# One copy and one guard for both heads in the attention core, and a norm's last square summed by TensorE

## What is computed

```python
def rmsnorm(x, g):
    y = x * lax.rsqrt(jnp.mean(x * x, axis=-1, keepdims=True) + EPS)
    return y * g

def attend_block(qb, keys, values, masks, sink):
    m = sink
    for s in scores:                       # 128 queries against up to 512 keys
        m = jnp.maximum(m, jnp.max(s, axis=-1))
    denom = jnp.exp(sink - m)
    for s, vp in zip(scores, values):
        p = jnp.exp(s - m[..., None])
        denom = denom + jnp.sum(p, axis=-1)
        out = out + p @ vp
    return out / denom

for i in range(4):                         # attention, pooling, Fourier, attention
    x = x + g1 * mixer_i(modulate(rmsnorm(x, norm_mix[i]), sh1, sc1))
    x = x + g2 * conv_ffn(modulate(rmsnorm(x, norm_ffn[i]), sh2, sc2))
```

## Time and profile before

| | |
|---|---|
| median of 3 runs | 2660.65 us (2658.5 to 2661.7) |
| the profiled execution | 2665.53 us, its span 2663.7 us |
| PE busy | 2573.9 us (97%) |
| DVE busy | 1984.8 us (75%) |
| ACT busy | 1299.1 us (49%) |
| POOL busy | 115.5 us (4%) |
| mean granted TensorE clock | 0.984 of full |

### The profile page before, as it was taken

One profiled execution on the slowest core, in us unless ns is written; L12 is line 12 of the kernel. 1 busy time (PEld: TensorE's weight loads), 2 busy tenths in 40 slices (PEclk: granted clock), 3 DMA queues, 4 the chain that ended last, 5 costly groups with the idle time before them and its releaser, 6 DMA issues.

```text
span 2663.7 us, 43103 instructions
## 1 busy us (share of the span) xinstructions
PE 2573.9 (97%) x15856; PEld 2383.5 (89%) x15856; DVE 1984.8 (75%) x3736; ACT 1299.1 (49%) x2291; POOL 115.5 (4%) x146
## 2 busy tenths in 40 slices
PE   6989999999998999999989999999998999999999
PEld 4966899999998999999879999999997699999998
DVE  3777488888896888888855888888868946754772
ACT  3467365425524663355244662454347936633551
POOL 2000100000012000000101000000100010000000
PEclk9999899999998999999989999999999999999999
DMA  7224122433341334434302335334320012222222
GB/s 292 64 95 148 58 101 104 163 138 118 108 168 48 103 110 160 154 105 146 124 21 72 116 111 184 111 110 153 118 71 29 2 56 72 78 87 64 76 83 78
DMA packets 72274, 279.64 MB, mean 105 GB/s; under 512 B 7888, under 2 KB 11344, under 8 KB 68560
## 3 DMA queue, kind: packets, MB, share of 16 engines
q1 hardware_dynamic: 72144, 277.93, 30.5%
HBM read 274.75 MB, written 3.15 MB: 104 GB/s over the span
## 4 chain that ended last, share of the span: by engine, by line
PE 89%; DVE 7%; issue 2%; ACT 1%; DMA 1%; POOL 0%; SPq 0%; DVEq 0%; ACTq 0%
PE ps L575 20%; PE ps L573 16%; PE ps L574 16%; PE ps L576 15%; PE ps L577 11%; PE ps L792 2%; PE ps L777 2%; PE ps L761 1%; PE ps L634 1%; DVE h L1406 1%; PE ps L687 1%; DVE prob L1609 1%; DVE ada_w L1352 1%; PE ps L828 1%; PE ps L569 1%
## 5 line engine op out<-in xcount | busy, mean ns | idle before, releaser
L575 PE MATMUL ps<-h,w_hi 128*128 128x512 f32 x1768 | 700.5, 396 | 0.0
L573 PE MATMUL ps<-h,w_hi 128*128 128x386 f32 x1768 | 604.8, 342 | 8.2 <-DVE h L1406 4.9
L574 PE MATMUL ps<-h,w_hi 128*128 128x386 f32 x1768 | 602.9, 341 | 0.0
L576 PE MATMUL ps<-h,w_lo 128*128 128x386 f32 x1768 | 598.7, 339 | 0.0
L950 ACT ACTIVATE tail<-ps 128x256 f32<-128x256 f32 x281 | 108.3, 386 | 966.0 <-PE ps L577 965.4
L577 PE MATMUL ps<-h,w_lo 128*128 128x256 f32 x1768 | 503.4, 285 | 0.0
L577 PEld LDWEIGHTS ps<-h,w_lo 128*128 128x128 f32 x1768 | 333.7, 189 | 79.6
L1293 DVE TENSOR_TENSOR w_lo<-w_raw,w_hi 128x1024 fp32r<-128x1024 f32 (+1 forms) x288 | 377.4, 1311 | 4.9 <-ACT w_hi L945 1.7
L573 PEld LDWEIGHTS ps<-h,w_hi 128*128 128x128 f32 x1768 | 339.3, 192 | 11.3 <-DVE h L1406 7.2
L574 PEld LDWEIGHTS ps<-h,w_hi 128*128 128x128 f32 x1768 | 335.8, 190 | 0.0
L575 PEld LDWEIGHTS ps<-h,w_hi 128*128 128x128 f32 x1768 | 334.0, 189 | 0.0
(11 more groups left out here) (166 smaller groups left out, 3890.0 us busy)
## 6 DMA issues: line engine op xcount, KB each, us to landing
w_raw<-in_w_in SPq DMA_DIRECT2D x176, 512.0 KB, 3.6
w_raw<-in_w_out SPq DMA_DIRECT2D x64, 704.0 KB, 4.1
ada_w<-in_ada_t SPq DMA_DIRECT2D x42, 1024.0 KB, 6.3
row_w<-in_ada_t SPq DMA_DIRECT2D x60, 512.0 KB, 3.5
ada_w<-in_ada_w SPq DMA_DIRECT2D x18, 1024.0 KB, 5.0
w_raw<-in_w_qkv SPq DMA_DIRECT2D x24, 512.0 KB, 3.5
w_raw<-in_w_o SPq DMA_DIRECT2D x16, 512.0 KB, 3.5
first_w<-in_ada_w SPq DMA_DIRECT2D x6, 1024.0 KB, 14.3
```

The lines of the kernel that those rows point to most:

```text
L573: pe.matmul(main, wh, b[:, 0, 0:MAIN], start=first, stop=False)
L574: pe.matmul(main, wh, b[:, 1, 0:MAIN], start=False, stop=False)
L575: pe.matmul(wide, wh, b[:, :, MAIN:NT], start=first, stop=last, skip_group_check=True)
L576: pe.matmul(main, wl, b[:, 0, 0:MAIN], start=False, stop=last)
```

## The change

In the attention core both heads share one guard, one count and one copy. `masked` issues the two mask-and-maximum operations first and then two small tensor operations of two columns each (a multiplication by `neg_scale`, a minimum with `neg_sink`); `max_made` counts once per work. `exps` waits once, for both heads. `turned` waits for the second head's `t_done` and makes one copy of both banks into a joint `probT`; `pt_made` counts once per work. In the two norms for which `explicit` is true POOL doesn't add the last square: it only counts, and PE sums `sq_sum` (seven tiles) and then, in the same PSUM columns, the last square itself.

```diff
@@ -178,7 +178,7 @@
             band = sb("band", [P, 640], F32, a)
             swapped = sb("swapped", [P, LAT], F32, a)
             prob = [sb(f"prob{s}", [P, 2, 516], F32, a) for s in range(2)]
-            probT = [[sb(f"probT{s}{hd}", [P, 512], F32, a) for hd in range(2)] for s in range(2)]
+            probT = [sb(f"probT{s}", [P, 2, 512], F32, a) for s in range(2)]
             prob.append(third_prob)
             stat = sb("stat", [P, 2, 2, 8], F32, a)
         with ExitStack() as a:
@@ -535,7 +535,10 @@
                         pool.wait_ge(sq_made, sq_base(layer, second) + kk + 1)
                         if kk > 1:
                             pool.wait_ge(sq_added, (KT - 1) * m + kk - 1)
-                        pool.tensor_tensor(sq_sum[:], sq_sum[:], sq[kk % 2][:], ALU.add).then_inc(sq_added, 1)
+                        if kk == KT - 1 and explicit(layer, second):
+                            pool.sem_inc(sq_added, 1)
+                        else:
+                            pool.tensor_tensor(sq_sum[:], sq_sum[:], sq[kk % 2][:], ALU.add).then_inc(sq_added, 1)
                     if KINDS[layer] == "attn" and not second:
 
                         a = layer // 3
@@ -626,12 +629,13 @@
                     first_tile(0, kk)
                     first_tile(1, kk)
 
-            def block_sums(src, sel, cols):
+            def block_sums(src, sel, cols, first=True, last=True):
 
                 for tb in range(5):
                     at = TOKEN_BLOCKS[tb]
                     c0 = SUMS.start + 2 * tb
-                    mm = pe.matmul(ps[:, INV_CTX, c0:c0 + cols], src[:, at:at + P], sel, start=True, stop=True)
+                    mm = pe.matmul(ps[:, INV_CTX, c0:c0 + cols], src[:, at:at + P], sel,
+                                   start=first and (last or tb == 0), stop=last, skip_group_check=first != last)
                 return mm
 
             def turn_back(r, cols=1):
@@ -645,12 +649,18 @@
 
             def sum_squares(layer, second):
                 m = 2 * layer + second
-                pe.wait_ge(sq_added, (KT - 1) * (m + 1))
+                lone = explicit(layer, second)
+                pe.wait_ge(sq_added, (KT - 1) * (m + 1) - lone)
                 if m:
                     pe.wait_ge(rstd_made, m)
                 if second and KINDS[layer] == "attn":
                     pe.wait_ge(ol_made, 40 * (layer // 3 + 1))
-                block_sums(sq_sum, ones[:], 1).then_inc(sum_done, 1)
+                if not lone:
+                    block_sums(sq_sum, ones[:], 1).then_inc(sum_done, 1)
+                    return
+                block_sums(sq_sum, ones[:], 1, last=False)
+                pe.wait_ge(sq_added, (KT - 1) * (m + 1))
+                block_sums(sq[(KT - 1) % 2], ones[:], 1, first=False).then_inc(sum_done, 1)
 
             def sum_heads(layer, i):
 
@@ -748,7 +758,7 @@
                         nb, tile = WORK[w - w0]
                         ga = tile // 4
                         if w - w0 >= 2:
-                            pe.wait_ge(max_made, 2 * (w - 1))
+                            pe.wait_ge(max_made, w - 1)
                         if w - w0 < 2:
                             wait_taken(pe, u0 + 10 + w - w0)
                         pe.wait_ge(qk_ready, 10 * a + tile + 3)
@@ -772,7 +782,7 @@
                             if w == w0:
                                 pe.wait_ge(q_root, KT * (a + 1))
                             if w - w0 >= 1:
-                                pe.wait_ge(pt_made, 2 * (w - 1) + hd + 1)
+                                pe.wait_ge(pt_made, w)
                             for b in BLOCKS[nb]:
                                 mm = pe.transpose(ps[:, 4 + hd, b * P:(b + 1) * P],
                                                   prob[w % 3][:, hd, b * P:(b + 1) * P], ident[:])
@@ -783,14 +793,14 @@
                         ga = tile // 4
                         if w - w0 >= 2 or (w > w0 and layer == 0):
                             pe.wait_ge(ol_made, w - 1 if layer else w)
-                        pe.wait_ge(pt_made, 2 * w + 2)
+                        pe.wait_ge(pt_made, w + 1)
                         for b in BLOCKS[nb]:
                             for hd in range(2):
                                 kv = slice(HD * (2 * ga + hd), HD * (2 * ga + hd + 1))
                                 own = KEYS[nb][0] <= b * P < KEYS[nb][1]
                                 v = v_tok[:, FIRST_KEYS[nb] + b - KEYS[nb][0] // P, kv] if own else cv[:, kv]
                                 mm = pe.matmul(out_bank(layer, w)[HD * hd:HD * hd + HD, :], v,
-                                               probT[w % 2][hd][:, b * P:(b + 1) * P],
+                                               probT[w % 2][:, hd, b * P:(b + 1) * P],
                                                start=(b == BLOCKS[nb][0]), stop=(b == BLOCKS[nb][-1]))
                         mm.then_inc(o_done, 1)
 
@@ -1095,9 +1105,9 @@
                         nb, tile = WORK[w - w0]
                         lo, hi = SPAN[nb]
                         act.wait_ge(sink_put, w + 1)
+                        act.wait_ge(max_made, w + 1)
                         for hd in range(2):
                             st = stat[:, w % 2, hd, :]
-                            act.wait_ge(max_made, 2 * w + hd + 1)
                             act.activation(prob[w % 3][:, hd, lo:hi + 1], prob[w % 3][:, hd, lo:hi + 1], ACT.Exp,
                                            bias=st[:, 1:2], scale=q_scale[:, tile, nb, hd:hd + 1],
                                            accum_out=st[:, 2:3]).then_inc(exp_made, 1)
@@ -1107,10 +1117,8 @@
                         b0, b1 = BLOCKS[nb][0] * P, (BLOCKS[nb][-1] + 1) * P
                         if w - w0 >= 2:
                             act.wait_ge(o_done, w - 1)
-                        for hd in range(2):
-                            act.wait_ge(t_done, 2 * w + hd + 1)
-                            act.activation(probT[w % 2][hd][:, b0:b1], ps[:, 4 + hd, b0:b1],
-                                           ACT.Copy).then_inc(pt_made, 1)
+                        act.wait_ge(t_done, 2 * w + 2)
+                        act.activation(probT[w % 2][:, :, b0:b1], ps[:, 4:6, b0:b1], ACT.Copy).then_inc(pt_made, 1)
 
                     def out_hi(w):
                         nb, tile = WORK[w - w0]
@@ -1610,12 +1618,12 @@
                                 out=prob[w % 3][:, hd, lo:hi], in0=ps[:, 2 * (w % 2) + hd, lo:hi],
                                 in1=band[:, (0 if nb == 3 else P) + lo:(0 if nb == 3 else P) + hi], scale=1.0, scalar=-3e38, op0=ALU.add, op1=ALU.max,
                                 accum_out=st[:, 0:1]))
-                            head = 8 * ga + 4 * hd + r
-                            if w - w0 < KT and hd == 0:
-                                dve.wait_ge(q_scaled, KT * a + tile + 1)
-                            dve.tensor_scalar(st[:, 1:2], st[:, 0:1], neg_scale[:, tile, nb, hd:hd + 1],
-                                              neg_sink[:, a, head:head + 1],
-                                              ALU.mult, ALU.min).then_inc(max_made, 1)
+                        st, head = stat[:, w % 2, :, :], 8 * ga + r
+                        if w - w0 < KT:
+                            dve.wait_ge(q_scaled, KT * a + tile + 1)
+                        own.link(dve.tensor_tensor(st[:, :, 1], st[:, :, 0], neg_scale[:, tile, nb, :], ALU.mult))
+                        dve.tensor_tensor(st[:, :, 1], st[:, :, 1], neg_sink[:, a, head:head + 5:4],
+                                          ALU.min).then_inc(max_made, 1)
 
                     def normed(w):
                         nb, _ = WORK[w - w0]
```

## The result

| | before | after |
|---|---|---|
| median, six runs each | 2661.19 us (2658.5 to 2663.4) | 2671.11 us (2667.15 to 2672.04) |
| ratio, 95% interval | | 1.0029 (1.0018 to 1.0040) |
| the profiled execution, its span | 2665.53, 2663.7 us | 2667.15, 2665.3 us |

Slower by 0.29%, 4.8 to 10.6 us; on the 2660.65 of the first runs that is 2668.4, where 2668.2 was predicted. The interval lies wholly above no change. The ratio is the one on record for the two sets of runs and isn't the quotient of the two medians, which is 1.0037; the median of after by itself is 2.9 us above the forecast.

What follows compares the result with a forecast made beforehand. TensorE held 89% of the chain; layer 3's core was bound by a loop through TensorE and ScalarE. Terms 9.6 + 1.0 - 2.6 - 0.4 = +7.6 on 2660.65 gave 2668.2 us, range 2662 to 2674.

Steps and rivals of the forecast that it cites:

- The loop of layer 3: Layer 3 core, transposes to copy to values: works go from 2.46 to 2.80 us (three blocks), 3.12 to 3.45 (four).
- half of the transposes: Layer 3 loop: the second head's transposes end 0.40 us (three blocks) or 0.51 us (four) later, delaying the copy.
- The sum for layer 3: Layer 3 core: 5.1 us from three-block works plus 5.3 from four-block works, less 0.8, makes +9.6 us.
- the seams: Layer 3 core, where scores change width: a few works already run slower than the loop, so 0.8 us is taken off.
- Layer 0: Layer 0 core: values wait for `out_lo`, so eight works lose 0.07 us each; +1.0 us in all, from 0 to 3.
- The guard at zero: VectorE's guard in the attention cores: 0.62 us a work before and after, so zero change.
- The norm ahead of pooling: Norm before pooling: PE sums the last square in a second pass of 1.3 us, root 2.6 us earlier, -2.6 us.
- The Fourier norm: Norm ahead of the Fourier mixer: the root waits only 0.42 us for PE, so -0.4 us and no more.
- A: Rival, attention cores: the copies' saved fixed part counts, 80 works by 0.06 us, ending faster at 2652.9 us; chance 0.05.
- B: Rival, attention cores: VectorE sets the pace and slack takes the lengthening; 2657.6 us, up to 2664 if half hidden; chance 0.15.
- C: Rival, attention cores: small waits drop TensorE's clock to 1.2 GHz, some 3 us per wider work, 2764 us; chance 0.01.
- D: Rival, norms: the second pass replaces the addition at the slow pace, root no earlier, 2671.2 us; chance 0.04.

Runs made afterwards that it cites:

- both copies late: Kernel before with one argument changed, so that both separate copies wait for the second head's transposes; ratio 1.0042 (1.0031 to 1.0053).
- the last experiment: Kernel after, with its wide copy, guard and norms, and VectorE's out_lo moved ahead of its normed; ratio 1.0010 (1.0000 to 1.0020), median 2663.37 us.

## Why the prediction was right, point by point

**The loop of layer 3** was read rightly, and one of its terms was 0.06 to 0.07 us too long. Copies of 0.81 and 1.02 us came out to the hundredth, 0.14 to the values and 0.81 and 1.03 to the next transposes also. Mis-sized was "half of the transposes", 0.40 and 0.51: the copy starts 0.34 and 0.44 later than before, 0.11 us for each block of the second head. I had taken 0.134 a block from the distance between the values and the next transposes. That distance holds a gap at the change of kind; the blocks of one run follow each other faster. So the works take 2.73 and 3.38 us, not 2.80 and 3.45, and a work costs 0.26, not 0.33.

**The sum for layer 3** was still near, 9.6 against 9.1. Added up by works, from the starts of the transposes: six three-block works +0.9 (three of them at +0.05, since they ran every 2.68 before), the sixteen of four blocks +4.8, eight three-block works +2.4, the last of one block -0.4. That is 7.7. The 30 wide ones by 0.26 would be 7.8, and they gave 8.1, with 0.6 in two late copies: so the seams took off 0.3 and not 0.8. The other 1.4 are the first two distances of the core, where the granted clock is still at its lower level of 1.2 GHz: for 10.2 us in before (2019.4 to 2029.6) and for 13.7 us in after (2011.2 to 2024.9), both windows with a clock of 0.50. In before the second work's transposes run at full speed, in after at half:

```profile
2030.34 0.87 PE L777 MATMUL ps<-ident,prob 128*128 128x128 f32 x6
```

```profile
2023.42 1.53 PE L787 MATMUL ps<-ident,prob 128*128 128x128 f32 x6
```

and in that of norms and guard without a wide copy too:

```profile
2017.38 1.54 PE L787 MATMUL ps<-ident,prob 128*128 128x128 f32 x6
```

This is also the +1.0 that this kernel shows for layer 3, so the longer stretch comes without the wide copy too. Whether it owes nothing to the change isn't shown: all four kernels that have lost the overlap (after, wide copy alone, both copies late, output first with all three) have it in layer 3, and of the six others this one alone. If it is chance, 7.7 of the 9.1 are the change's, and that 9.6 came so near is in part luck.

The two late copies are one in the four-block works and one in the last three-block works, each 0.28 us behind its neighbours, in every kernel with the wide copy. What holds them up wasn't found.

**Layer 0** was priced at +1.0 and came out at 0.0. The wait for `out_lo` hid the copy as foreseen (2.35 against 2.36 us to the values). Alone the copy costs 0.7 there. What I hadn't seen is that the guard shortens VectorE's way to `out_lo`, by 0.1 a work, worth 2.1 us alone; in after it buys nothing, since the copy's own loop of 3.38 stands where the old wait stood. The two aren't additive: -2.1 and +0.7 make 0.0, and not -1.4. The 0.0 itself holds 0.8 us of the lower clock in the first two works (8.39 us for their two distances in after, 7.57 in before); from the third work on after is 0.8 us shorter. So the sign of the +1.0 wasn't confirmed either. The -2.1 of the guard alone holds +1.0 of the same kind.

**The guard at zero** was nearly right. A work costs VectorE 0.12 + 0.12 + 0.19 + 0.08 = 0.51 us, not 0.62. The failed term is the last 0.19: I priced the step from the second small operation to the reciprocal as a linked one, but the reciprocal doesn't read the guard. It is worth 0.1 in the works of one block, 0.4 us in layer 3.

**The norm ahead of pooling** gained 2.2 where 2.6 was predicted. The second pass took 1.83 us, not 1.3. The granted clock fell while it ran; windows of after ahead of and behind that point, then of the norms alone:

```profile
814.80:816.40 1.60, 0.54 (x5) 0.45 (x5) 1.57 (x4) 1.47 (x3) 0.00 (x0) 1.00 0.00 0
816.60:818.00 1.40, 1.18 (x6) 1.09 (x6) 0.00 (x0) 0.71 (x2) 0.00 (x0) 0.50 0.52 85
```

```profile
813.20:814.50 1.30, 1.25 (x10) 1.19 (x10) 0.59 (x3) 1.22 (x1) 0.00 (x0) 1.00 0.00 0
```

At the 2.4 GHz level throughout it is 1.28, at 1.2 GHz it was 2.27; in after TensorE had been without work for 1.06 us when the pass began, as in the other, and only the moment of the fall differs. In the six profiles with the norms' part the stage gained 2.2 to 2.7, and 2.7 in three of them; the 0.4 of the guard alone in that stage is of the same kind, as nothing of the guard lies there. `gain` took 0.17 us (1.51 before): without POOL's addition beside it nothing holds it up, as the rule on VectorE and POOL's shared ports in the Trainium skill (SBUF — State Buffer, "SBUF: two separate sides") would have it. The eight splits of the tables ahead of the Fourier mixer tell the same: before, beside POOL's addition, and after:

```profile
1330.09 4.12 DVE L1520 TENSOR_TENSOR tab_lo<-tab_raw,tab_hi 128x258 fp32r<-128x258 f32 x8
```

```profile
1326.67 2.79 DVE L1528 TENSOR_TENSOR tab_lo<-tab_raw,tab_hi 128x258 fp32r<-128x258 f32 x8
```

This saving earns nothing, since ScalarE's table load ends at 1330.09 and the root starts at 1330.11. **The Fourier norm** gained its 0.44, all of the wait that there was.

**The rivals.** A fell: ScalarE has 80 instructions fewer, and the wide copy alone costs 12.8 us (9 to 16). In its condition stands a slip: for three blocks the wide copy would have to end in 2.46 - 0.64 - 0.40 - 0.14 - 0.81 = 0.47 us and not 0.41; against a copy of 0.81 it changes nothing. The rule on large tiles (VectorE: DVE Perf Modes, "The TRN2 errata", in the Trainium skill) is stated there for operands in SBUF, while these copies read PSUM. The rows agree with it in direction, 0.06 us a work from both copies late to the wide copy; the overlap that pays for it is five times that. B, that slack takes the lengthening, held in layer 0, where the sum had already priced it at +1.0, and not in layer 3; the last experiment shows that slack to be the wait for `out_lo`. C fell: TensorE waits 0.19 us for the copy in the four-block work shown and 0.63 in the three-block one, and the clock is 1.00 in the window of the earlier trace rows and from 2100 to 2119, among the three-block works, where TensorE is busy for 16.07 of 19 us. The lower level at the start of each core stands in the profile of before too. D fell: the norms alone gain 2.7.

**The total** came nearer than its terms. The stages add up to +6.5 where +7.6 was forecast: layer 3 was priced 0.5 too high, layer 0 1.0 too high, and the norm ahead of pooling gained 0.4 less. Of the 6.5, 1.4 and 0.8 are the lower clock in the first works of the two cores; without these the sum would be 4.3. The mechanism, the lost overlap in layer 3, was right: it shows wherever the overlap is gone (wide copy alone, both copies late) and goes when it is put back (everything but the wide copy). That the total lies so near the forecast is in part luck.

## What to carry to other kernels

Before two instructions on a consumer are merged, look at what the producer does during the first: if the second half of its output is made then, and the consumer's end is on the loop that sets the period, the merge costs that half's production time and saves one fixed part. A stage that is covered by another wait shows no loss and no gain, so a profile of one part alone, or the sum of such, doesn't tell what the parts do together; the wait to look for is the one that stands at the same instant. Here moving one operation of VectorE ahead of another (the output's low part ahead of the normalisation) took the kernel with the norms' part from -2.7 to -9.9 us, which is about what the whole change lost.

## What the runs showed of the hardware

TensorE has stretches at the lower granted clock that stand in one profile and not in another, in a part of the program that the change doesn't touch. In the profile of before two windows in layer 2 have 0.96 and 0.91:

```profile
1360.00:1400.00 40.00, 36.18 (x243) 32.55 (x242) 19.92 (x51) 17.23 (x47) 0.00 (x0) 0.96 0.04 14
1440.00:1460.00 20.00, 18.64 (x102) 17.32 (x101) 13.83 (x31) 9.62 (x22) 1.56 (x1) 0.91 0.20 75
```

and in that of after both are at 1.00:

```profile
1360.00:1400.00 40.00, 36.16 (x240) 32.81 (x239) 17.42 (x42) 15.86 (x41) 1.73 (x1) 1.00 0.09 27
1440.00:1460.00 20.00, 18.79 (x112) 17.67 (x111) 13.50 (x24) 11.80 (x18) 0.64 (x1) 1.00 0.16 54
```

The part from the first Fourier product to the core of layer 3 takes 674.9 us in after and 678.4 in before. These 3.5 us are most of the 4.9 by which the difference of the two spans, 1.6, falls short of the stages' 6.5. The other profiles agree: that part takes 678.3 to 678.5 us in the four that have both low stretches (before, norms alone, the two with separate copies and the output first), 676.4 with one (guard alone) and 674.9 to 675.3 in the five with none, so each costs some 1.7 us. Since each profile is of another kernel, it isn't shown that they are chance: all four kernels without the overlap are among the five.

For an effect of a few microseconds the spans of two executions can't be subtracted, but their stages can, where no such stretch falls inside.
